# Two transformer blocks on one core: a 512-column moving operand in the MLP's up projections, and steps moved at the first norm, in the mix stage, at the FFN's end and in the last norm

## The chip, the core and the metric

The kernel runs on one core of a Trainium2 chip. Times are device microseconds of an execution of the whole program. The core's engines are TensorE (PE; its weight loads are shown as PEld), VectorE (DVE), ScalarE (ACT), GpSimd (POOL) and SyncE (SP, which here only issues DMAs). Each runs its own instructions in order and waits for the others by semaphores.

## The reference, cut to what matters

```python
def reference(x, ...):                       # x is 1 x 256 x 1024, fp32
    h = rms_norm(x, mix_pre_norm)
    mix = hybrid_token_mixer(h, w_in, ...)   # window attention, block attention, gated delta rule
    x = x + rms_norm(mix, mix_post_norm)
    x = x + rms_norm(conv_glu_ffn(rms_norm(x, ffn_pre_norm), ...), ffn_post_norm)   # width 2816
    h = x
    for l in range(2):
        hn = rmsnorm(h, norm_mix_g[l])
        h = h + (gmlp_mixer(hn, ...) if l == 0 else mla_mixer(hn, kv, ...))
        h = h + sq_relu_mlp(rmsnorm(h, norm_mlp_g[l]), mlp_w1[l], mlp_w2[l])
        if l == 0: kv = shared_latent_kv(h, ...)
    return rmsnorm(h, final_norm_g)

def sq_relu_mlp(hn, w1, w2):                 # w1 1024 x 4096, w2 4096 x 1024
    return jnp.square(jax.nn.relu(hn @ w1)) @ w2
def rms_norm(x, w): return x * lax.rsqrt(jnp.mean(x * x, -1, keepdims=True) + 1e-6) * w
```

## The kernel before, in words

**Products in three parts.** Weights and activations are fp32. Each is split into a high part rounded to fp32r, the operand type that TensorE takes in one pass, and a low part that holds the rest: `w = w_hi + w_lo`, `h = hT_hi + hT_lo`. A product is the sum of hi x hi, lo x hi and hi x lo; `mm3` (L240 to L242) issues these three matmuls into one place of PSUM. Smaller products in the attention parts are plain fp32, which the trace shows as two passes for each matmul.

**Units.** All weights stream from HBM in units of 1 MB (128 x 2048 fp32), in three slots (`raw`) that are refilled in turn. `load` on SyncE waits until a slot's unit has been split, `split_hi` (L204) on ScalarE makes w_hi once the unit has landed and TensorE has used the unit three before, and `split_lo` (L218) on VectorE makes w_lo from it. TensorE waits for `lo_ready`.

**Stages.** They are mix, ffn, gmlp, mlp0, mla and mlp1, in this order. The 256 tokens are two blocks of 128. X (tokens on the partitions) is normalized, turned by TensorE into hT (8 tiles of 128 features x 256 tokens), and multiplied. From the second stage on the scale of a norm is applied to the sums afterwards, and only the first and the last norm scale rows themselves: `norm_act`, `norm_dve`, `norm_pool`. At the start ScalarE squares X in four halves (L358), VectorE adds two sums (L390), GpSimd raises the mean to -1/2 (L420, `n_rstd`), and each engine multiplies half of each block (L362, L403). Then ScalarE and VectorE split unit 0 as a whole, and make hT_hi (L382) and hT_lo (L412) tile by tile. PE runs warming matmuls of the identity (`warm`, L329) in its gaps.

**MLP stages** (`plain_pe`, `plain_act`, `plain_dve`; 544 us on and 814 us on). 16 pairs, each of 2 x 128 hidden features. An up unit (`up`, `features`) forms 2 tiles of 128 features x 256 tokens: for each tile 8 k steps of `mm3` with 256 columns of hT, 48 matmuls, both tiles in the halves of one bank. ScalarE takes the relu (L701), VectorE squares it (L731, act_f), ScalarE rounds act_hi (L706), VectorE makes act_lo (L736). A down unit (`down`) adds the pair's part to four banks (ACC) with 24 matmuls of 512 columns; it is run one pair later, behind the next up unit, for which TensorE waits on `pair_lo`. The splits of two weight units stand between these steps on ScalarE and VectorE. Pairs 2 to 13 run in loops of three pairs.

**Mix stage.** Its units are named by what they project: QB, K0, K1, ZB, KB, VB and so on. SyncE loads QB, K0 and K1 as units 0 to 2; ZB (unit 3) brings 8 more columns, 1,024 pieces of 32 bytes. `first_taps` on ScalarE (it needs `par`, the transposed parameters) and `other_taps` on VectorE (L2221) are the convolution of a key unit, `silu` closes it (L2075), and `rows_out` (L1788) turns the keys back. GpSimd issues the DMAs of masks, small parameters and the alibi table. Later the levels of a triangular inverse run on TensorE (`products`, L1798) among projections and attention groups: `at_scale` multiplies probabilities (ScalarE, L2059), `at_turn` transposes them; `zs` holds the gate z. L1938 sums the squared queries: 8 matmuls of 8 columns.

**Borders.** `ffn_act`'s `ending` is the last pair of the FFN; after it come `post_act` (L509), `post_dve` (L523, L528, L534) and `post_pool` (L516), the norm of the FFN's output. `final_dve` (L930) scales the last rows and `final_sync` writes them.

## Time and profile before

| | us |
|---|---|
| median of 3 runs | 991.94 (989.93 to 992.95) |
| profiled execution | 990.83 |
| its span, first to last instruction | 989.0 |
| TensorE busy in the span | 968.7 |
| VectorE busy | 641.3 |
| ScalarE busy | 500.6 |
| HBM read | 163.26 MB |

The mean granted clock of TensorE is 0.997. Busy is the union of an engine's instructions; a printed duration of a matmul reaches until its end, while the next one starts earlier, so costs are read from start to start. In a row of the timeline, `[0.52 <-ACT union L2171]` is the idle time before it and what ended it; `x4` is a number of merged instructions. 128x256 is partitions x elements per partition.

### The profile page before, as it was taken

The page shows a single profiled execution, that of the slowest core. Times are in us where ns is not written, and L with a number is a line of the kernel's source. Part 1 is how long each engine was busy: PE and PEld are TensorE (multiplying, and loading weights), DVE is VectorE, ACT ScalarE, POOL GpSimd, SP SyncE. Part 2 cuts the span into 40 slices and gives each one's busy share as a digit, 9 for nine tenths or more (in the row PEclk, how much of TensorE's full clock was granted, in tenths as well). Part 3 has the DMA queues.
Part 4 walks back from the last instruction along what each step waited for, and adds up shares of the span by engine and source line. Part 5 has one row for each costly group of instructions (what it writes and reads, how often), then busy time and mean ns, then how long its engine had stood idle before and what let it go on. Part 6 is the DMA issues. An engine that isn't in the chain of part 4 may idle for free.

```text
span 989.0 us, 16482 instructions
## 1 busy us (share of the span) xinstructions
PE 968.7 (98%) x6739; PEld 901.2 (91%) x6739; DVE 641.3 (65%) x803; ACT 500.6 (51%) x666; POOL 35.1 (4%) x46
## 2 busy tenths in 40 slices
PE   7999999999999999999999999999999999999996
PEld 7999998899999998999999999999899899999995
DVE  5666757687777777587668654555767665454553
ACT  5765464565454556444336434434656464434432
POOL 1000001200000000000001000001000000000000
PEclk9999999999999999999999999999999999999998
DMA  9933213466565545555455565655464446565641
GB/s 280 246 114 122 85 44 96 148 226 213 170 205 177 183 158 155 186 170 171 171 170 184 183 200 177 205 170 186 124 159 171 128 145 218 178 203 176 206 129 42
DMA packets 128590, 165.04 MB, mean 167 GB/s; under 512 B 20862, under 2 KB 111419, under 8 KB 128411
## 3 DMA queue, kind: packets, MB, share of 16 engines
q1 hardware_dynamic: 127067, 159.57, 50.1%
q0 software_dynamic: 1312, 4.68, 1.6%
q8 instruction: 37, 0.61, 0.2%
q14 instruction: 14, 0.11, 0.0%
q10 hardware_dynamic: 160, 0.07, 0.0%
HBM read 163.26 MB, written 1.05 MB: 166 GB/s over the span
## 4 chain that ended last, share of the span: by engine, by line
PE 90%; DVE 4%; ACT 2%; DMA 2%; issue 1%; POOL 0%; POOLq 0%; SPq 0%; DVEq 0%; ACTq 0%
PE ps L240 27%; PE ps L241 27%; PE ps L242 27%; PE ps L1798 2%; PE ps L1177 1%; DMA raw<-in_w_in_dram 1%; DVE w_lo L218 1%; PE ps L1198 1%; ACT w_hi L204 1%; PE ps L1064 1%; PE ps L1793 1%; DVE union L2221 1%; PE ps L451 1%; PE ps L1187 0%; DMA X<-in_x_dram 0%
## 5 line engine op out<-in xcount | busy, mean ns | idle before, releaser
L218 DVE TENSOR_TENSOR w_lo<-raw,w_hi 128x2048 fp32r<-128x2048 f32 (+2 forms) x149 | 338.9, 2276 | 164.2 <-ACT w_hi L204 164.2
L204 ACT ACTIVATE w_hi<-raw 128x2048 fp32r<-128x2048 f32 (+2 forms) x149 | 283.3, 1902 | 137.6 <-PE ps L242 130.4
L240 PE MATMUL ps<-hT_hi,w_hi 128*128 128x256 f32 x1192 | 339.7, 285 | 2.0 <-DVE hT_lo L412 1.6
L241 PE MATMUL ps<-hT_hi,w_lo 128*128 128x256 f32 x1192 | 337.2, 283 | 0.0
L242 PE MATMUL ps<-hT_lo,w_hi 128*128 128x256 f32 x1192 | 337.2, 283 | 0.0
L240 PEld LDWEIGHTS ps<-hT_hi,w_hi 128*128 128x128 f32 x1192 | 228.4, 192 | 4.6 <-issue 1.3
L241 PEld LDWEIGHTS ps<-hT_hi,w_lo 128*128 128x128 f32 x1192 | 228.5, 192 | 1.7
L242 PEld LDWEIGHTS ps<-hT_lo,w_hi 128*128 128x128 f32 x1192 | 228.4, 192 | 0.0
L240 PE MATMUL ps<-w_hi,act_hi 128*128 128x512 f32 x416 | 163.3, 392 | 0.0
L241 PE MATMUL ps<-w_hi,act_lo 128*128 128x512 f32 x416 | 162.4, 390 | 0.0
L242 PE MATMUL ps<-w_lo,act_hi 128*128 128x512 f32 x416 | 162.0, 389 | 0.0
L242 PEld LDWEIGHTS ps<-w_lo,act_hi 128*128 128x128 f32 x416 | 78.1, 188 | 16.7
L240 PEld LDWEIGHTS ps<-w_hi,act_hi 128*128 128x128 f32 x416 | 78.3, 188 | 14.9
L241 PEld LDWEIGHTS ps<-w_hi,act_lo 128*128 128x128 f32 x416 | 78.3, 188 | 14.4
L240 PE MATMUL ps<-w_hi,hT_hi 128*128 128x256 f32 (+3 forms) x256 | 81.1, 317 | 2.0 <-DVE hT_lo L412 0.8
L242 PE MATMUL ps<-w_lo,hT_hi 128*128 128x256 f32 (+3 forms) x256 | 79.2, 309 | 0.0
L241 PE MATMUL ps<-w_hi,hT_lo 128*128 128x256 f32 (+3 forms) x256 | 79.1, 309 | 0.0
L701 ACT ACTIVATE act_tmp<-ps 128x512 f32<-128x512 f32 x32 | 19.1, 598 | 108.7 <-PE ps L242 108.7
L731 DVE TENSOR_TENSOR act_f<-act_tmp 128x512 f32<-128x512 f32 x32 | 22.1, 691 | 58.3 <-ACT act_tmp L701 58.3
L240 PEld LDWEIGHTS ps<-w_hi,hT_hi 128*128 128x128 f32 x256 | 48.8, 190 | 5.3 <-issue 2.4
L242 PEld LDWEIGHTS ps<-w_lo,hT_hi 128*128 128x128 f32 x256 | 48.7, 190 | 2.7
L241 PEld LDWEIGHTS ps<-w_hi,hT_lo 128*128 128x128 f32 x256 | 48.8, 191 | 2.2
(298 smaller groups left out, 899.6 us busy)
## 6 DMA issues: line engine op xcount, KB each, us to landing
raw<-in_mlp_w_dram SPq DMA_DIRECT2D x64, 1024.0 KB, 5.3
raw<-in_w_up_dram SPq DMA_DIRECT2D x22, 1024.0 KB, 5.1
raw<-in_a_w_in_dram SPq DMA_DIRECT2D x16, 1024.0 KB, 5.3
raw<-in_w_in_dram SPq DMA_DIRECT2D x12, 1024.0 KB, 6.6
raw<-in_w_down_dram SPq DMA_DIRECT2D x11, 1024.0 KB, 4.9
raw<-in_a_w_out_dram SPq DMA_DIRECT2D x8, 1024.0 KB, 4.8
raw<-in_w_out_dram SPq DMA_DIRECT2D x4, 1024.0 KB, 5.0
raw<-in_b_w_o_dram SPq DMA_DIRECT2D x4, 1024.0 KB, 5.0
```

The source lines that it names most:

```text
L204: nc.scalar.activation(w_hi[:, s, 0:n], raw[:, r, 0:n], ACT.Copy).then_inc(hi_ready, 1)
L218: nc.vector.tensor_tensor(w_lo[:, s, 0:n], raw[:, r, 0:n], w_hi[:, s, 0:n].bitcast(F32), ALU.subtract).then_inc(lo_ready, 1)
L240: nc.tensor.matmul(o, a[0], b[0], start=start, stop=False, skip_group_check=shared)
L241: nc.tensor.matmul(o, a[1], b[0], start=False, stop=False, skip_group_check=shared)
L242: return nc.tensor.matmul(o, a[0], b[1], start=False, stop=stop, skip_group_check=shared)
L451: mm = pe.transpose(turned(n, t)[:, tb * P:(tb + 1) * P], X[:, tb, t * P:(t + 1) * P], ident[:])
L701: nc.scalar.activation(act_tmp[:, m, :], W[m][:], func).then_inc(f.t, 1)
L731: nc.vector.tensor_tensor(act_f[:, m, :], act_tmp[:, m, :], by, ALU.mult).then_inc(f.f, 1)
L1064: mm = nc.tensor.matmul(W[3][:, t * S + tb * P:t * S + (tb + 1) * P], gv[:, tb, c:c + P], wsT[:, p, :], start=True, stop=True)
L1177: mm = nc.tensor.matmul(o, qs[m], ks[m], start=m == 0, stop=m == len(qs) - 1)
L1198: mm = nc.tensor.matmul(o, gr.v(h, kb), PT[:, kb, h, :], start=kb == 0, stop=kb == gr.tb)
L1798: mm = nc.tensor.matmul(bank[:, hs], a[:, g, :], b[:, g, :], start=True, stop=True)
```

## The change

It has six parts.

1. **Up units of the MLP.** hT_hi and hT_lo lie side by side for each tile (`hT[:, k, 0 or 1, :]`), so that both are one moving operand of 512 columns. `up_halves` runs, for each k, w_lo x hT_hi of 256 columns for tile 0 and for tile 1, then w_hi x [hT_hi, hT_lo] of 512 columns for tile 0 and for tile 1. A tile has a bank of its own, and successive matmuls go to the two banks in turn. A bank's left half holds hi x hi, its right half the rest. ScalarE copies the right half, VectorE adds the left one, and one operation takes relu and square. The pairs run in loops of six (SyncE's too). Pair 0 is computed as before.
2. **First norm and unit 0.** ScalarE squares and scales block 0, VectorE block 1, 1024 wide; GpSimd adds epsilon. Unit 0 comes in two DMAs of 4 k tiles and is split by halves, as unit 1 is; units 0 and 1 are multiplied k by k (`up_by_tile`). 8 warming matmuls on zeros stand ahead of the identity's arrival.
3. **Start of the mix stage.** ScalarE loads the silu table by a 1-element activation; the parameter copy and the first taps stand ahead of the splits of ZB and KB; VectorE's taps stand ahead of them too. ZB's narrow DMA is issued ahead of its wide one. GpSimd's DMAs wait for ZB and KB.
4. **Inverse's products.** The 8 sums of squared queries go one by one among the last products, behind waits for the squares and the probabilities' copies; `at_scale` of the last group moves behind the squares and the copy of zs.
5. **FFN's end.** `split_hi(act, u + 4)` stands ahead of the two act_hi copies.
6. **Last norm.** VectorE multiplies halves 0 to 2 by the gains as they close; then the scales are applied by both engines, and four DMAs of half a block write the result, one from ScalarE's queue. The last down unit takes `down_by_block`'s order.

The core of the diff:

```diff
+        def up_halves(b, u):
+            w_h, w_l = weights(u, KT)
+            for k in range(KT):
+                for t in range(PAIR):
+                    nc.tensor.matmul(banks[:, b + t, S:2 * S], w_l[:, k, t * P:(t + 1) * P], hT[:, k, 0, :], start=k == 0, stop=False,
+                                     skip_group_check=True)
+                for t in range(PAIR):
+                    mm = nc.tensor.matmul(banks[:, b + t, :], w_h[:, k, t * P:(t + 1) * P], hT[:, k, :, :].rearrange("p x s -> p (x s)"),
+                                          start=False, stop=k == KT - 1, skip_group_check=True)
+            mm.then_inc(unit_used, 1)
...
+        def mlp_act(act, f, n, extra=None):
...
+                    nc.scalar.copy(tiles2(act_tmp, m % 3), banks[:, b:b + 2, S:2 * S]).then_inc(f.t, 1)
+                if not last:
+                    split_hi(act, u + 3, 2 * i)
...
+        def mlp_dve(dve, f, n, extra=None):
...
+                    nc.vector.tensor_tensor(tiles2(act_tmp, m % 3), banks[:, b:b + 2, 0:S], tiles2(act_tmp, m % 3),
+                                            ALU.add).then_inc(f.z, 1)
...
+                    nc.vector.scalar_tensor_tensor(act_f[:, m % 3, :], z, 0.0, z, ALU.max, ALU.mult).then_inc(f.f, 1)
...
+        def start_norm_dve(dve, gain):
...
+            half_split_lo(dve, 0, 0)
+            dve.wait_ge(g_ok, 1)
+            norm_lo(dve, 0, gain, tiles=range(0, 4))
+            half_split_lo(dve, 0, 1)
+            norm_lo(dve, 0, gain, tiles=range(4, KT))
+            half_split_lo(dve, 1, 0)
+            half_split_lo(dve, 1, 1)
...
+                split_hi(act, u + 4)
                 for t in range(PAIR):
                     c = slice(t * S, (t + 1) * S)
                     act.wait_ge(f.f, j + 1 + t)
                     nc.scalar.copy(act_hi[:, m, c], g[:, c]).then_inc(f.hi, 1)
-                split_hi(act, u + 4)
...
-            pool.wait_ge(landed[1], landed_at[1])
+            pool.wait_ge(landed[ZB % RAW], landed_at[ZB])
...
-            pool.wait_ge(landed[2], landed_at[2])
+            pool.wait_ge(landed[KB % RAW], landed_at[KB])
...
+            def products_and_sums(bank, a, b, tb, done, first):
+                for h, g, hs in heads(tb):
+                    mm = nc.tensor.matmul(bank[:, hs], a[:, g, :], b[:, g, :], start=True, stop=True)
+                    if first == h // 2:
+                        sums = nc.tensor.matmul(ps[6][:, 8 * g:8 * g + 8], sqT[:, h, tb * P:(tb + 1) * P], onec[:], start=True, stop=True)
...
             nc.scalar.copy(qbT, ps[0][:].rearrange("p (t s) -> p t s", t=2)).then_inc(e_p, 1)
+            nc.scalar.activation(stat[:, 15:16], stat[:, 0:1], ACT.Silu)
+            start_act(act)
+            first_taps(0, False)
             split_hi(act, u0 + QB + 3)
-            start_act(act)
-            first_taps(0)
+            split_hi(act, u0 + K0 + 3)
             first_taps(1)
...
-            at_scale(act, gs[3])
             act.wait_ge(d_si, 3)
             nc.scalar.activation(sqT, qT, ACT.Square).then_inc(d_si, 1)
             act.wait_ge(unit_used, u0 + Z1 + 1)
             nc.scalar.copy(zs[:, :, UC:2 * UC], ps[1][:].rearrange("p (b c) -> p b c", b=TB)).then_inc(e_p, 1)
+            at_scale(act, gs[3])
```

On TensorE, at the head of an up unit in a loop of the first MLP, the program had these rows (ps2 is a bank, `pair_t` the relu of the pair before):

```order
L240 MATMUL ps2<-hT_hi,w_hi 128x256 [waits pair_t]
L241 MATMUL ps2<-hT_hi,w_lo 128x256
L242 MATMUL ps2<-hT_lo,w_hi 128x256
L240 MATMUL ps2<-hT_hi,w_hi 128x256
L241 MATMUL ps2<-hT_hi,w_lo 128x256
```

In the changed kernel the same place reads (`ps` is now one tensor of all eight banks):

```order
L863 ISA [waits lo_ready]
L851 MATMUL ps<-hT,w_lo 128x256 [waits pair_f]
L851 MATMUL ps<-hT,w_lo 128x256
L854 MATMUL ps<-hT,w_hi 128x512 x2
L851 MATMUL ps<-hT,w_lo 128x256 x2
L854 MATMUL ps<-hT,w_hi 128x512 x2
```

Three matmuls of 256 columns for a tile and k became one of 256 and one of 512, tile 0 and tile 1 in turn.

On VectorE, at the start of the program, from the first norm to the second unit's low part, before:

```order
L390 SCALAR_TENSOR_TENSOR stat<-stat 128x1 [waits n_sq]
L403 TENSOR_SCALAR XN<-X,stat 128x512 [waits n_rstd]
L390 SCALAR_TENSOR_TENSOR stat<-stat 128x1 [waits n_sq]
L403 TENSOR_SCALAR XN<-X,stat 128x512 [waits n_rstd]
L218 TENSOR_TENSOR w_lo<-raw,w_hi 128x2048 [waits hi_ready]
L412 SCALAR_TENSOR_TENSOR hT_lo<-ps4,par,hT_hi 128x256 [waits n_hi,g_ok]
```

and in the changed kernel:

```order
L401 SCALAR_TENSOR_TENSOR act_tmp,stat<-X 128x1024 [waits x_in1]
L404 TENSOR_SCALAR XN<-X,stat 128x1024 [waits n_rstd]
L248 TENSOR_TENSOR w_lo<-raw,w_hi 128x1024 [waits half_hi]
L491 SCALAR_TENSOR_TENSOR hT<-ps,par,hT 128x256 [waits n_hi,g_ok]
L491 SCALAR_TENSOR_TENSOR hT<-ps,par,hT 128x256 [waits n_hi] x3
L248 TENSOR_TENSOR w_lo<-raw,w_hi 128x1024 [waits hi_ready]
L491 SCALAR_TENSOR_TENSOR hT<-ps,par,hT 128x256 [waits n_hi] x4
```

The first hT_lo tile (L412, now L491) stands behind half of unit 0's low part, the second half between tiles 3 and 4.

On VectorE behind the last matmul, before (ps6 and ps7 are the sums of the second block, L501 closes the residual):

```order
L501 SCALAR_TENSOR_TENSOR X<-ps6,stat,X 128x512 [waits acc_done]
L501 SCALAR_TENSOR_TENSOR X<-ps7,stat,X 128x512 [waits unit_used]
L390 SCALAR_TENSOR_TENSOR stat<-stat 128x1 [waits n_sq]
L930 SCALAR_TENSOR_TENSOR act_tmp<-X,stat,rows 128x1024 [waits n_rstd,rows_in]
L930 SCALAR_TENSOR_TENSOR act_tmp<-X,stat,rows 128x1024 [waits n_rstd]
```

and in the changed kernel (L581 closes the residual):

```order
L581 SCALAR_TENSOR_TENSOR X<-ps,stat,X 128x512 [waits acc_done]
L581 SCALAR_TENSOR_TENSOR X<-ps,stat,X 128x512 [waits unit_used]
L446 TENSOR_TENSOR act_tmp<-X,rows 128x512 [waits x_done]
L450 SCALAR_TENSOR_TENSOR stat<-stat 128x1 [waits n_sq]
L465 TENSOR_SCALAR act_tmp<-act_tmp,stat 128x512 [waits o_z,n_rstd]
L467 SCALAR_TENSOR_TENSOR act_tmp<-X,stat,rows 128x512 [waits n_rstd]
```

One 512-wide operation (L467) stands behind the second power where a 1024-wide one (L930) stood.

## Rows read from the trace of the kernel before

**Rows 1.** The page's part 1 (busy time) and part 4 (chain by engine).

```profile
PE 968.7 (98%) x6739; PEld 901.2 (91%) x6739; DVE 641.3 (65%) x803; ACT 500.6 (51%) x666; POOL 35.1 (4%) x46
...
PE 90%; DVE 4%; ACT 2%; DMA 2%; issue 1%; POOL 0%; POOLq 0%; SPq 0%; DVEq 0%; ACTq 0%
```

**Rows 2.** First MLP: length; busy PE, PEld, DVE, ACT, POOL; PEclk, DMA share, GB/s.

```profile
544.00:689.00 145.00, 145.00 (x934) 132.69 (x933) 79.39 (x63) 62.81 (x52) 0.22 (x1) 1.00 0.58 188
```

**Rows 3.** Timeline of TensorE, first MLP: start us, us, engine, line, operation.

```profile
600.22 0.28 PE L240 MATMUL ps<-hT_hi,w_hi 128*128 128x256 f32 x1
...
605.98 0.40 PE L240 MATMUL ps<-w_hi,act_hi 128*128 128x512 f32 x1
...
611.44 0.28 PE L240 MATMUL ps<-hT_hi,w_hi 128*128 128x256 f32 x1
...
695.74 0.40 PE L240 MATMUL ps<-w_hi,act_hi 128*128 128x512 f32 x1
...
705.29 0.92 PE L451 MATMUL ps<-ident,X 128*128 128x128 f32 x7
```

**Rows 4.** Timeline of ScalarE and VectorE beside that pair.

```profile
606.17 0.60 ACT L701 ACTIVATE act_tmp<-ps 128x512 f32<-128x512 f32 x1 [3.84 <-PE ps L242]
...
606.67 1.91 ACT L204 ACTIVATE w_hi<-raw 128x2048 fp32r<-128x2048 f32 x1
...
606.80 0.69 DVE L731 TENSOR_TENSOR act_f<-act_tmp 128x512 f32<-128x512 f32 x1 [2.14 <-ACT act_tmp L701]
...
608.61 2.29 DVE L218 TENSOR_TENSOR w_lo<-raw,w_hi 128x2048 fp32r<-128x2048 f32 x1 [1.11 <-ACT w_hi L204]
...
610.82 0.68 DVE L736 TENSOR_TENSOR act_lo<-act_f,act_hi 128x512 fp32r<-128x512 f32 x1
```

**Rows 5.** Weight transfers (L187) from 810 to 970 us: issue to landing.

```profile
DMA to landing us min/median/max: 4.8/5.2/7.6
```

**Rows 6.** The chain of waits at the start: start us, us, what.

```profile
0.74 3.90 DMA X<-in_x_dram
...
9.11 0.72 ACT XN L362
...
11.73 2.30 DVE w_lo L218
...
14.49 13.99 DMA raw<-in_w_in_dram
```

**Rows 7.** Timeline of TensorE and GpSimd at the start.

```profile
5.38 2.93 PE L329 MATMUL ps<-ident 128*128 128x128 f32 x12
...
11.47 2.40 PE L329 MATMUL ps<-ident 128*128 128x128 f32 x20
...
14.56 0.36 PE L240 MATMUL ps<-hT_hi,w_hi 128*128 128x256 f32 x1 [0.69 <-DVE hT_lo L412]
...
40.45 1.09 PE L1788 MATMUL ps<-ident,union 128*128 128x128 f32 x8 [1.47 <-ACT union L2075]
...
43.49 0.24 POOL L1757 TENSOR_SCALAR dd<-dd 128x8 f32<-128x8 f32 x1 [27.42 <-DVE dd L2245]
```

**Rows 8.** As rows 2, from 40 to 180 us, the mix stage.

```profile
40.00:180.00 140.00, 138.74 (x1096) 130.95 (x1097) 93.73 (x160) 78.44 (x146) 7.50 (x6) 1.00 0.35 108
```

**Rows 9.** Timeline of TensorE late in the mix stage.

```profile
134.44 0.66 PE L1788 MATMUL ps<-ident,union 128*128 128x128 f32 x4 [0.52 <-ACT union L2171]
...
142.34 1.95 PE L1938 MATMUL ps<-onec,XN 128*128 128x8 f32 x16
```

**Rows 10.** Timeline at the end of the FFN.

```profile
368.93 2.29 DVE L218 TENSOR_TENSOR w_lo<-raw,w_hi 128x2048 fp32r<-128x2048 f32 x1 [1.39 <-ACT w_hi L204]
...
370.15 0.19 ACT L509 ACTIVATION_READ_ACCUMULATOR act_tmp<-ps 128x1 f32 x1
```

**Rows 11.** Timeline behind the last matmul.

```profile
983.13 1.53 POOL L420 TENSOR_TENSOR stat<-stat,mhalf 128x1 f32<-128x1 f32 x1 [2.09 <-DVE stat L390]
...
984.69 1.28 DVE L930 SCALAR_TENSOR_TENSOR act_tmp<-X,stat,rows 128x1024 f32<-128x1024 f32 x1 [0.44 <-POOL stat L420]
```

More of the change, by code:

```diff
@@ L649, in __init__ @@
                     self.r = pair_r if st == "gmlp" else None
+                    self.z = pair_z
+                    self.zbase = sum(f.pairs - 1 for n, f in before.items() if n != "gmlp")
         def each_pair(eng, f, per, step, u_of, ending=None):
             bodies = (f.pairs - 2) // per
-            looped = bodies if bodies > 2 else 0
+            looped = bodies if bodies * per > 6 else 0
             step(1, 1, u_of(1), 0)
@@ L688, in plain_pe @@
             else:
-                down(u, (tiles2(act_hi, m), tiles2(act_lo, m)), last=True)
+                down_by_block(pe, u, (tiles2(act_hi, m), tiles2(act_lo, m)))
         def plain_act(act, f, per, func, n, extra=None):
@@ new lines, in mlp_pe, with step @@
+        def mlp_pe(pe, f, n):
+            def step(j, m, u, i):
+                one = isinstance(j, int) and j == 1
+                pe.wait_ge(lo_ready, u + 1 + 2 * i * PERIOD)
+                if not one:
+                    pe.wait_ge(f.f, f.base + j - 1)
+                up_halves(2 * (m % 2), u)
+                pe.wait_ge(f.lo, f.base + j)
+                pe.wait_ge(lo_ready, u + 2 + 2 * i * PERIOD)
+                down(u + 1, (tiles2(act_hi, (m - 1) % 3), tiles2(act_lo, (m - 1) % 3)), first=one)
+            each_pair(pe, f, 6, step, lambda j: f.u0 + 2 * j - 1)
+            u = f.u0 + 2 * f.pairs - 1
+            acts = (tiles2(act_hi, (f.pairs - 1) % 3), tiles2(act_lo, (f.pairs - 1) % 3))
+            pe.wait_ge(f.lo, f.base + f.pairs)
+            pe.wait_ge(lo_ready, u + 1)
+            if n + 1 in UNSCALED:
+                down_by_half(pe, u, acts, n + 1)
+            else:
+                down_by_block(pe, u, acts)
@@ L2523, in _ @@
                 else:
[L2524 to L2525 removed]
+                    split_lo(dve, SPL - 1)
                 if st == "mix":
```

327 lines of the change are left out of this document (205 added, 122 removed).

## The prediction

> **What bounds the kernel now.** I read the page's first part and its chain first. TensorE is busy 98% of the span and the chain that ended last runs on it for 90% [rows 1]: outside a few borders a change pays only if it takes TensorE's own time, and at a border it pays what it takes from the chain. So I asked three things: what one matmul costs from start to start inside the two MLP stages, whether the other engines have room there, and what stands on the chain at the first norm, in the mix stage, at the end of the FFN and after the last matmul.
>
> The MLP stages have no holes. From 544 to 689 us TensorE is busy 145.00 of 145.00 us at a granted clock of 1.00, its 2.4 GHz level [rows 2]. One pair takes 11.22 us (600.22 to 611.44): an up unit of 48 matmuls of 256 columns in 5.76 us, then a down unit of 24 of 512 columns in 5.46 us [rows 3]. Start to start that is 119.9 ns at 256 columns and 227.6 ns at 512. Twice the columns cost 107.7 ns more, so 256 columns are 107.7 ns and 12.2 ns stand on every matmul whatever its width. The printed durations (0.28 and 0.39 us) hold the part that overlaps the next matmul and are not used.
>
> **The wide operand.** Per tile and k the change runs one matmul of 256 columns and one of 512 in place of three of 256: 32 matmuls in an up unit for 48, over the same 12,288 columns. 16 x 119.9 + 16 x 227.6 ns = 5.56 us for 5.76: 0.20 us less. Pairs 1 to 15 of each stage use it (pair 0 keeps the old form), so 30 x 0.20 = 5.9 us go. That the two widths are mixed, and that every matmul goes to another bank than the one before, no row shows. The nearest rows: in a down unit the bank changes after every third matmul (227.6 ns), in the last unit of a stage after every sixth. The 42 matmuls from 695.74 to 705.29 us take 9.55 us [rows 3]; less 5.46 for the first 24, the 18 others take 227.1 ns each. One changes bank in 1 of 3, the other in 1 of 6, for 0.5 ns: at most 3 ns a change, 960 changes, 2.9 us. On the other side a cost of 12.2 ns that vanished wherever the bank changes would give 960 x 12.2 = 11.7 us more. I take no effect, the value of the rows that lie together, and keep 3.0 and 17.6 us gained as the ends of this term.
>
> The Trainium skill, "TensorE: Matmul & The Clock Gate", section "Wait — 56ns, not 53.3ns?", speaks against this edit: it puts the fixed cost of a warm matmul at about 2.5 ns, by which 480 fewer matmuls would be worth 1.2 us in all. The trace has 12.2 ns, nearly five times that (the section measured bf16 matmuls, these read fp32r), so the measurement decides.
>
> **Who must keep up.** A tile's product now lies in two halves of a bank, so ScalarE copies one half (before: relu of all, 0.60 us) and VectorE adds the other and then squares: one more VectorE operation a pair, 0.69 us by L731 [rows 4]. VectorE needs 2 x 2.29 + 0.69 + 0.68 = 6.0 of 11.2 us a pair and gets 6.7 of 11.0. The added one is hidden: ScalarE's split of the next weights (L204, from 606.67, 1.91 us) runs meanwhile and its act_hi copy stands behind it, so act_lo still ends 5.4 us after the unit (611.5), and TensorE asks for it only at 617.2, behind the next up unit. In the last pair no split stands between: 0.60 + 0.69 + 0.75 + 0.61 + 0.68 = 3.3 us, against a down unit of 5.46. Weights land in 4.8/5.2/7.6 us (least, median, most) [rows 5], two transfers in 11.0 us. Loops of six pairs in place of three: units start 11.22 us apart across the old loop's ends too, so that is worth nothing.
>
> **First norm and unit 0.** X's first block lands at 4.64 us; four squares, two powers, two half-wide multiplications (the last until 9.83), then w_hi and w_lo (2.30) of the whole unit 0 [rows 6], hT_lo tiles only behind them, and the first product at 14.56 [rows 7]. New: ScalarE has block 0. One square of 1024 (about 1.25), an added GpSimd sum (0.24, as L1757 [rows 7]) and a power (0.56): rstd at 6.9; its multiplication of 1024, 0.72 and a little over half again, ends at 8.1. VectorE has block 1, landed near 6.1: 1.28 for the square (1024 wide, as L930 [rows 11]), GpSimd 0.9, multiplication 0.9: 9.2, where the old one ended at 9.83. Half of unit 0 is split by ScalarE from 8.1 to 9.2 and by VectorE from 9.3 to 10.5; the first hT_hi tile ends at 10.8, its hT_lo at 11.2, and tiles follow every 0.4 us while TensorE wants one every 0.72. VectorE's second half stands between tiles 3 and 4 and ends near 13.7; TensorE needs it at 11.3 + 2.9 = 14.2. So the first product moves from 14.56 to about 11.3: 3.3 us. Unit 1 (split by halves, the first until 16.6; unit 0 ends at 17.1) and unit 2 (until 20.1, needed at 22.9) stay in time.
>
> TensorE's clock matters here: the first 12 warming passes take 0.22 us each (half rate, the 1.2 GHz level), the 20 from 11.47 us 0.12 (full) [rows 7]. New warming passes begin near 1 us, so I take the full level from about 8; if it comes at 11, the turns end 1.4 us later and the term is 2.0.
>
> Behind it TensorE waits 1.47 us at 40.45 for the silu of the keys [rows 7]. Its cause is the DMA: unit 3 takes 13.99 us to land [rows 6], since GpSimd's table and alibi transfers run beside its 1,024 pieces of 32 bytes, and ScalarE waits for it until 28.48 with the parameter copy and the first taps queued behind. Now those stand ahead of the split, VectorE's taps ahead of its own, the silu table is loaded early, and GpSimd's transfers wait until units 3 and 4 have landed. I put unit 3 near 22 us against a need at 24.5. Unit 2 is multiplied by 28.9, ZB's w_lo ends at 29.2 and its products at 35.6, the keys' silu at 33: the 1.47 goes. 3.3 + 1.5 = 4.8; I take 4.6, for a chain this long seldom loses nothing. Ends: 1.5 (a late clock and a late unit 3) and 5.5.
>
> **Mix.** ScalarE's scaling of the last probabilities now stands behind the square of the queries and the copy of zs, for which TensorE waits 0.52 us at 134.44 [rows 9]. The copy comes 1.7 us earlier and the scaling, done near 134.1, is just in time for the turn: 0.5. The 16 passes of query sums (1.88 us from 142.34, 117 ns each for 8 columns, so bound by their weight loads) go between the products. The loads stay one to a pass, so I take 0; ends: 1.0 slower (ScalarE's copies of the products start later) and 1.0 faster.
>
> **FFN's end.** VectorE's w_lo, from 368.93 until 371.2, keeps L523 from its first product, whose square was there at 370.34 [rows 10]. The split now goes into ScalarE's idle time from 364.2, so w_lo ends near 369.8, L523 starts 0.8 us earlier, and the two means and closings behind it, for which TensorE waits, 0.5. It delays the first act_hi copy by 0.8, to 366.5; act_lo, at 367.0, is still there before TensorE ends the unit ahead. Ends 0 and 0.8.
>
> **Last norm.** The last data is ready at 984.69 + 1.28 = 985.97 [rows 11]. Now the gains are multiplied in early, and behind the second power stand one 512-wide VectorE operation (0.7) and one on ScalarE. The last closing moves to 982.5 (0.4 later, three operations ahead of it), the last square ends at 983.3, the power at 984.1 to 984.5 (it took 1.53 us beside L930), the last half at 985.1: 0.9, and a transfer is half as large: 1.0. Ends 0.2 and 1.6.
>
> **Sum.** 5.9 + 4.6 + 0.5 + 0.5 + 1.0 = 12.5 us. The profiled execution took 990.83 us (span 989.0 and 1.8 around it), which gives 978.3; the median of the runs shown, 991.94, is 1.1 above it: 979.4.
>
> **Rivals.** A: the start's gain is given back before the FFN, the mix being a weave of TensorE, VectorE and ScalarE steps whose units load only when their slots are split. Against: from 40 to 180 us TensorE is busy 138.74 of 140 us [rows 8], so little else leads. If half or all of it goes: 981.7 to 984. B: a wide matmul costs two narrow ones when mixed with them, 239.8 ns, and the edit brings nothing: 979.4 + 5.9 = 985.3. Against: 24 in a row take 227.6 each. The skill's 2.5 ns, named above, would end nearly there, at 984.1. C: alternating banks removes the fixed cost: 979.4 - 11.7 = 967.7; the 3 ns point the other way. D, slower: a matmul into another bank than its predecessor's waits for it. Place: the 960 of the wide units. It takes 13 ns a change to undo the whole gain and 16 to be seen as slower; at 20 ns the time is 979.4 + 19.2 = 998.6. For it is only that no row has a change at every matmul; against it, 3 ns a change. E: the second half of unit 0 or unit 3 comes late and the wide units bring nothing either: 990.
>
> **Chances.** Forecast 0.63, A 0.17, B 0.06, C 0.07, D 0.03, E 0.04. About 0.3%, 3 us, can be told from no change here. Faster by more: 0.63 + 0.17 + 0.06 + 0.07 = 0.93; same 0.04; slower 0.03. The range holds the forecast's own (976 to 982.5), A's and nearly B's: 975 to 985.
>
> **What would show it.** Right: pairs of 11.02 us in both MLP stages with TensorE busy throughout, starts 120 and 228 ns apart; the first product near 11.3 us and no wait ahead of the keys' turns, none for zs; the FFN's L523 no longer behind w_lo; the last output operation 0.9 us nearer to the last matmul. Wrong: a pair above 11.15 or below 10.9, TensorE waiting for pair_lo or for weights inside an MLP stage, a first product after 12.5 us, or a mix stage that is longer than before from the keys' turns to its last unit.

## The result, and the profile after

The changed kernel takes 978.19 us (median, 978.03 to 978.42) against 991.89 us (989.93 to 992.95) for the kernel before, timed beside it: a ratio of 0.987 (95% interval 0.986 to 0.988). Forecast were 979.4 us and 975 to 985. The profiled execution took 978.03 us, its span is 976.0: 13.0 us shorter.

Page of the changed kernel, parts 1 and 4, to be laid beside [rows 1]:

```profile
PE 961.9 (99%) x6269; PEld 874.1 (90%) x6269; DVE 663.4 (68%) x838; ACT 500.4 (51%) x664; POOL 34.8 (4%) x48
...
PE 95%; DVE 2%; ACT 1%; issue 1%; DMA 0%; POOL 0%; POOLq 0%; DVEq 0%; ACTq 0%
```

TensorE lost 470 matmul records and 6.8 us of busy time, VectorE gained 22 us (mostly the added operation, 30 x 0.69), and the chain now runs on TensorE for 95% in place of 90%. Where the 13.0 us went I read by laying the same operation of both timelines side by side: the distance of each pair, and by how much it grew.

| place | before | after | apart | gained there |
|---|---|---|---|---|
| first product | 14.56 | 11.95 | 2.61 | 2.6 |
| keys' turns | 40.45 | 35.95 | 4.50 | 1.9 |
| mix, a `products` of the inverse | 119.63 | 115.07 | 4.56 | 0.1 |
| mix, the turn that waited for zs | 134.44 | 129.21 | 5.23 | 0.7 |
| mix, first `state_out` | 144.22 | 138.58 | 5.64 | 0.4 |
| FFN, last down unit | 361.95 | 356.27 | 5.68 | 0.0 |
| FFN's end, second turn | 376.72 | 370.37 | 6.35 | 0.7 |
| first MLP, its turns | 526.20 | 519.87 | 6.33 | 0.0 |
| its end, the next turns | 705.29 | 695.90 | 9.39 | 3.1 |
| second MLP, last down unit but one | 970.24 | 957.86 | 12.38 | 3.0 |
| end of the span | 989.0 | 976.0 | 13.0 | 0.6 |

**Inside the MLP.** The stretch of [rows 2] in the changed kernel (length; busy PE, PEld, DVE, ACT, POOL; PEclk, DMA share, GB/s), and the heads of two up and two down units, to be laid beside [rows 3]:

```profile
544.00:689.00 145.00, 145.00 (x738) 123.31 (x737) 92.14 (x74) 65.26 (x57) 3.69 (x1) 1.00 0.58 190
```

```profile
603.71 0.40 PE L851 MATMUL ps<-hT,w_lo 128*128 128x256 f32 x2
...
609.28 0.39 PE L270 MATMUL ps<-w_hi,act_hi 128*128 128x512 f32 x1
...
614.72 0.40 PE L851 MATMUL ps<-hT,w_lo 128*128 128x256 f32 x2
...
620.30 0.39 PE L270 MATMUL ps<-w_hi,act_hi 128*128 128x512 f32 x1
```

An up unit takes 5.57 to 5.58 us for 5.76, a down unit 5.44 for 5.46, a pair 11.01 for 11.22, without a hole. Beside them ScalarE's copy, VectorE's addition and square, and the split, in the place of [rows 4]:

```profile
598.47 0.59 ACT L888 COPY act_tmp<-ps 128x512 f32<-128x512 f32 x1 [3.66 <-PE ps L854]
598.95 1.92 ACT L219 ACTIVATE w_hi<-raw 128x2048 fp32r<-128x2048 f32 x1
599.09 0.69 DVE L912 TENSOR_TENSOR act_tmp<-ps,act_tmp 128x512 f32<-128x512 f32 x1 [1.95 <-ACT act_tmp L888]
599.82 0.69 DVE L916 SCALAR_TENSOR_TENSOR act_f<-act_tmp 128x512 f32<-128x512 f32 x1
...
603.11 0.69 DVE L920 TENSOR_TENSOR act_lo<-act_f,act_hi 128x512 fp32r<-128x512 f32 x1
```

act_lo is there at 603.8 us, TensorE asks for it at 609.28: the added operation is hidden with 5.5 us to spare.

**The start.** Timeline of ScalarE, VectorE, GpSimd and TensorE, for [rows 6, 7]:

```profile
5.35 2.27 PE L361 MATMUL ps<-ident 128*128 128x128 f32 x18
...
6.10 1.23 DVE L401 SCALAR_TENSOR_TENSOR act_tmp<-X 128x1024 f32<-128x1024 f32 x1 [5.06 <-DMA X<-in_x_dram]
6.38 1.38 POOL L420 TENSOR_TENSOR stat<-stat,mhalf 128x1 f32<-128x1 f32 x1
...
7.79 1.15 ACT L391 ACTIVATE XN<-X,stat 128x1024 f32<-128x1024 f32 x1 [1.84 <-POOL stat L420]
...
8.15 0.57 POOL L420 TENSOR_TENSOR stat<-stat,mhalf 128x1 f32<-128x1 f32 x1
...
9.08 1.94 PE L546 MATMUL ps<-ident,XN 128*128 128x128 f32 x16 [1.46 <-ACT XN L391]
...
11.95 0.35 PE L270 MATMUL ps<-hT,w_hi 128*128 128x256 f32 x1
```

The first of two equal powers takes 1.38 us, the second 0.57. The granted clock is at its full level, 2.4 GHz, from 4.44 us (a pass behind it takes 0.126 us); in the kernel before it was there from 11.27.

**The tail.** Timeline behind the last matmul, for [rows 11]:

```profile
970.94 0.49 DVE L465 TENSOR_SCALAR act_tmp<-act_tmp,stat 128x512 f32<-128x512 f32 x1
971.09 0.73 POOL L497 TENSOR_TENSOR stat<-stat,mhalf 128x1 f32<-128x1 f32 x1 [1.70 <-DVE stat L450]
...
971.86 0.75 DVE L467 SCALAR_TENSOR_TENSOR act_tmp<-X,stat,rows 128x512 f32<-128x512 f32 x1 [0.44 <-POOL stat L497]
972.61 0.39 ACTq L440 DMA_DIRECT2D out_dram<-act_tmp  x1
972.64 0.33 SPq L1110 DMA_DIRECT2D out_dram<-act_tmp  x1
```

The last data is ready at 972.61, 13.36 us earlier than at 985.97, but the span ends 3.39 us behind it where it ended 3.03 behind. The trace has the landing of the last transfer 2.92 us after its issue (972.64 to 975.56, 256 KB, with those issued at 971.85 and 972.61 still under way); before, it was 2.64 (986.01 to 988.64, 512 KB, alone).

### The profile page after: what moved, and what is told of

The parts are those of the page before. It is cut to its first block, busy times and chain, and to the rows that moved or that the text cites. A ratio compares the mean times of both kernels' runs of the same rounds, so it can differ in the third digit from the quotient of the medians.

```text
span 976.0 us, 15567 instructions
## 1 busy us (share of the span) xinstructions
PE 961.9 (99%) x6269; PEld 874.1 (90%) x6269; DVE 663.4 (68%) x838; ACT 500.4 (51%) x664; POOL 34.8 (4%) x48
## 3 DMA queue, kind: packets, MB, share of 16 engines
HBM read 163.26 MB, written 1.05 MB: 168 GB/s over the span
## 4 chain that ended last, share of the span: by engine, by line
PE 95%; DVE 2%; ACT 1%; issue 1%; DMA 0%; POOL 0%; POOLq 0%; DVEq 0%; ACTq 0%
PE ps L270 23%; PE ps L272 22%; PE ps L271 22%; PE ps L854 11%; PE ps L851 6%; PE ps L1972 2%; PE ps L1351 2%; PE ps L1372 1%; PE ps L1967 1%; PE ps L1238 1%; PE ps L532 1%; PE ps L1361 0%; PE ps L2101 0%; DMA X<-in_x_dram 0%; PE ps L2121 0%
## 5 line engine op out<-in xcount | busy, mean ns | idle before, releaser
L233 DVE TENSOR_TENSOR w_lo<-raw,w_hi 128x2048 fp32r<-128x2048 f32 x147 | 334.3, 2276 | 133.7 <-ACT w_hi L219 133.7
L219 ACT ACTIVATE w_hi<-raw 128x2048 fp32r<-128x2048 f32 x147 | 279.9, 1904 | 129.7 <-PE ps L272 128.4
L270 PE MATMUL ps<-hT,w_hi 128*128 128x256 f32 x712 | 203.7, 286 | 1.4 <-DVE hT L491 0.9
L271 PE MATMUL ps<-hT,w_lo 128*128 128x256 f32 x712 | 201.4, 283 | 0.0
L272 PE MATMUL ps<-hT,w_hi 128*128 128x256 f32 x712 | 201.4, 283 | 0.0
L854 PE MATMUL ps<-hT,w_hi 128*128 128x512 f32 x480 | 150.8, 395 | 0.0
L270 PEld LDWEIGHTS ps<-hT,w_hi 128*128 128x128 f32 x712 | 136.4, 192 | 2.8 <-issue 1.5
L271 PEld LDWEIGHTS ps<-hT,w_lo 128*128 128x128 f32 x712 | 136.5, 192 | 0.6
L272 PEld LDWEIGHTS ps<-hT,w_hi 128*128 128x128 f32 x712 | 136.4, 192 | 0.0
L851 PEld LDWEIGHTS ps<-hT,w_lo 128*128 128x128 f32 x480 | 90.0, 188 | 20.9
L851 PE MATMUL ps<-hT,w_lo 128*128 128x256 f32 x480 | 94.5, 278 | 0.0
L270 PE MATMUL ps<-w_hi,hT 128*128 128x256 f32 (+3 forms) x256 | 81.1, 317 | 1.9 <-DVE hT L491 0.8
L272 PE MATMUL ps<-w_lo,hT 128*128 128x256 f32 (+3 forms) x256 | 79.2, 309 | 0.0
L271 PE MATMUL ps<-w_hi,hT 128*128 128x256 f32 (+3 forms) x256 | 79.1, 309 | 0.0
L854 PEld LDWEIGHTS ps<-hT,w_hi 128*128 128x128 f32 x480 | 73.1, 189 | 0.0
L888 ACT COPY act_tmp<-ps 128x512 f32<-128x512 f32 x30 | 17.7, 589 | 100.4 <-PE ps L854 100.4
```

Source lines behind the costliest of these rows:

```text
L219: nc.scalar.activation(w_hi[:, s, 0:n], raw[:, r, 0:n], ACT.Copy).then_inc(hi_ready, 1)
L233: nc.vector.tensor_tensor(w_lo[:, s, 0:n], raw[:, r, 0:n], w_hi[:, s, 0:n].bitcast(F32), ALU.subtract).then_inc(lo_ready, 1)
L270: nc.tensor.matmul(o, a[0], b[0], start=start, stop=False, skip_group_check=shared)
L271: nc.tensor.matmul(o, a[1], b[0], start=False, stop=False, skip_group_check=shared)
L272: return nc.tensor.matmul(o, a[0], b[1], start=False, stop=stop, skip_group_check=shared)
L851: nc.tensor.matmul(banks[:, b + t, S:2 * S], w_l[:, k, t * P:(t + 1) * P], hT[:, k, 0, :], start=k == 0, stop=False, skip_group_check=True)
```

## The experiments

All are edits of the changed kernel and compute the same output. Times are medians; runs 5 to 8 have one execution each. The changed kernel was timed in the first set only. The kernel before was timed beside every set, and its median lay between 990.30 and 991.89 us, so differences below about 1 us are read from the traces and not from the times.

**1. Narrow matmuls again, all else kept (`e1_narrow`).**

```diff
-                    mm = nc.tensor.matmul(banks[:, b + t, :], w_h[...], hT[:, k, :, :]...)
+                for x in range(2):
+                    for t in range(PAIR):
+                        mm = nc.tensor.matmul(banks[:, b + t, x * S:(x + 1) * S], w_h[...], hT[:, k, x, :], ...)
```

> The changed kernel, but in the MLP's wide up units the one matmul of 512 columns (w_hi x [hT_hi, hT_lo]) is two of 256, into the left and the right half of the same bank; tiles, banks, copies, additions, splits and order stay: 48 matmuls a unit for 32, the same 12,288 columns, and nearly every matmul still goes to another bank than the one before. Theory F (a fixed cost of about 12.2 ns on each matmul): a pair takes 11.22 us again for 11.02, 30 pairs, +5.9 us: 978.2 + 5.9 = 984.1, TensorE without holes. Rival B' (the 5.9 us came from another part of the change, for instance from the loops of six pairs or from the two banks): pair stays 11.02 us, 978.2. Rival D' (changing the bank at each matmul costs time that the wide form hid): pair above 11.3 us, over 986.5.

984.24 us (983.92 to 984.37). Heads of two up units and the down unit between them:

```profile
605.05 0.40 PE L851 MATMUL ps<-hT,w_lo 128*128 128x256 f32 x2
...
610.80 0.40 PE L270 MATMUL ps<-w_hi,act_hi 128*128 128x512 f32 x1
...
616.27 0.40 PE L851 MATMUL ps<-hT,w_lo 128*128 128x256 f32 x2
```

A pair is 11.22 us again (up 5.75, down 5.47), so the step of the width alone is worth 6.1 us. The loops of six, the two banks and the other form of relu and square together are worth nothing. B' and D' are out.

**2. One bank after the other (`e2_one_bank`).**

```diff
-            for k in range(KT):
-                for t in range(PAIR): (w_lo, 256 columns)
-                for t in range(PAIR): (w_hi, 512 columns)
+            for t in range(PAIR):
+                for k in range(KT): (w_lo, 256 columns), (w_hi, 512 columns)
```

> The changed kernel, but the MLP's wide up units run tile 0 over all eight k (256 and 512 columns in turn, all into one bank) and then tile 1 into the other bank: one change of bank in 32 matmuls in place of one at nearly every matmul; same matmuls, same number. Theory F (bank does not matter, the cost is per matmul and per column): pair 11.02 us, 978.2 within 0.6. Rival C' (alternating banks saves a part of the gain): pair longer, by up to 0.20 us, up to 984. Rival D' (alternating banks costs): pair shorter, by up to 3 ns x 32 = 0.10 us, down to 975.3.

980.95 us (980.68 to 981.18): +2.8. Heads of two units, TensorE's timeline:

```profile
604.93 0.28 PE L851 MATMUL ps<-hT,w_lo 128*128 128x256 f32 x1
...
610.57 0.40 PE L270 MATMUL ps<-w_hi,act_hi 128*128 128x512 f32 x1
...
616.03 0.28 PE L851 MATMUL ps<-hT,w_lo 128*128 128x256 f32 x1
```

The up unit takes 5.64 us, the pair 11.11: nearly half of the gain is lost to an order of the same 32 matmuls. Theory F (only number and columns count) falls. It looked like C', but two things had changed together: the bank, and that 256 and 512 columns now alternate at every matmul (in the changed kernel they come two and two). Runs 9 to 11 part them.

**3. 384 and 128 columns for 512 (`e3_uneven`).**

```diff
-                    mm = nc.tensor.matmul(banks[:, b + t, :], w_h[...], hT[:, k, :, :]...)
+                for c in (slice(0, 384), slice(384, 512)):
+                    for t in range(PAIR):
+                        mm = nc.tensor.matmul(banks[:, b + t, c], w_h[...], hh[:, c], ...)
```

> The changed kernel, but the wide matmul of 512 columns is one of 384 and one of 128 (a up unit has then 16 matmuls of 256, 16 of 384 and 16 of 128 columns: 48, and 12,288 columns). From 119.9 ns at 256 and 227.6 ns at 512 columns two readings are possible. Theory F (12.2 ns on each matmul + 0.421 ns a column): 119.9 + 173.8 + 66.1 = 359.7 ns a tile and k, the same as three of 256: pair 11.22 us, time 984.1. Rival L (a matmul takes at least as long as its weight load, near 117 ns by the query sums, and 256 columns happen to lie near that floor): 119.9 + 173.8 + 117 = 410.7 ns, unit 6.57 us, pair 12.03, +30 us: about 1008.5. Between the two, a smaller floor: the pair's length gives the price of 128 columns.

1006.15 us (1006.04 to 1006.74): 28.0 us more than the changed kernel, and 21.9 more than run 1, which has as many matmuls and columns. Head of an up unit and of the next down unit:

```profile
610.24 0.40 PE L851 MATMUL ps<-hT,w_lo 128*128 128x256 f32 x2
...
616.65 0.45 PE L270 MATMUL ps<-w_hi,act_hi 128*128 128x512 f32 x1
```

6.41 us for 16 groups of 256, 384 and 128 columns: 400.6 ns each. Less 119.9 and 173.8 (interpolated) that leaves 106.9 ns for 128 columns, where the line through 256 and 512 gives 66. So rival L holds in kind, and the trace shows where: from 560 to 680 us no two weight loads of TensorE (its rows PEld) start less than 107 ns apart, close to the 117 ns a pass of the query sums [rows 9]. It is a floor of the loads, not of each matmul. Start to start the first of two matmuls of 128 columns takes 60 ns and the second 111, and the first of 256 columns behind them 164 for 119.9: short matmuls leave the next loads uncovered. At 256 columns the floor lies just below. The line 12.2 ns + 0.421 ns a column is good from 256 to 512 columns (384 take 174.6 here, 173.8 by the line), and not below. The down units of this run are also 0.1 us longer (5.54); why, no run tells.

**4. Another division of the first norm (`e4_swap`).**

```diff
-            act.wait_ge(n_rstd, 1)
-            nc.scalar.mul(XN[:, 0, :], X[:, 0, :], stat[:, 6:7]).then_inc(n_xa, 1)
+            act.wait_ge(x_in[1], 16)
+            nc.scalar.activation(act_tmp[:, 2:4, :]..., X[:, 1, :], ACT.Square, ..., accum_out=stat[:, 2:3]).then_inc(n_sv, 1)
...
-            nc.vector.scalar_tensor_tensor(act_tmp[...], X[:, 1, :], 1.0 / D, X[:, 1, :], ...)
+            dve.wait_ge(n_rstd, 1)
+            nc.vector.tensor_scalar(XN[:, 0, :], X[:, 0, :], stat[:, 6:7], None, ALU.mult).then_inc(n_xa, 1)
```

> The changed kernel with another division of the first norm: ScalarE squares both blocks (block 1 where it multiplied block 0), VectorE squares none and multiplies both blocks by their scales (tensor_scalar, 0.75 us each for ScalarE's 1.15). Theory P (GpSimd's power took 1.38 us for 0.57 because it stood blocked until VectorE's square of block 1, an operation with two SBUF inputs, ended at 7.34): the first power takes about 0.57 us again and ends at 6.95, XN of block 0 is there at 7.7 (8.94 before), block 1's at 9.0 (9.5), w_hi of unit 0 starts at 7.4 (8.85), the first product comes near 10.9 us for 11.95, and about 1.0 us of it reaches the end: 977.2 (976.8 to 977.9). Rival Q (the first power is slow by itself, as the first of its kind or through what GpSimd loads): it stays at 1.38 us, XN of block 0 at 8.5, first product 11.5, 977.8. Rival R (the time ahead of ZB is set by DMA landings, so nothing of it lasts): first product earlier, the keys' turns still at 35.95, 978.2.

978.00 us (977.33 to 978.25): nothing that can be told from 978.19. Its timeline shows why:

```profile
5.35 4.21 PE L361 MATMUL ps<-ident 128*128 128x128 f32 x18
...
6.39 0.57 POOL L420 TENSOR_TENSOR stat<-stat,mhalf 128x1 f32<-128x1 f32 x1
6.99 0.75 DVE L402 TENSOR_SCALAR XN<-X,stat 128x1024 f32<-128x1024 f32 x1 [5.94 <-POOL stat L420]
...
9.08 1.06 ACT L242 ACTIVATE w_hi<-raw 128x1024 fp32r<-128x1024 f32 x1 [0.45 <-DMA raw<-in_w_in_dram]
...
9.35 2.07 PE L546 MATMUL ps<-ident,XN 128*128 128x128 f32 x16
```

P is right on the power (0.57 us) and Q is out: XN of block 0 is ready at 7.74. But two waits took its place. In this execution the granted clock came to 2.4 GHz only at 9.66 us, so the 18 warming passes took 4.21 us, and the turns stood behind them; and unit 0's second half lands at 9.08, with hT_hi queued behind its w_hi on ScalarE. The first product came at 12.07.

**5 and 6. The power alone; unit 0's low part in one piece (`e5_lone_power`, `e6_whole_unit0`).**

```diff
+            dve.wait_ge(n_rstd, 1)                  # 5: ahead of VectorE's square
```
```diff
             half_split_lo(dve, 0, 0)
+            half_split_lo(dve, 0, 1)                # 6: both halves ahead of the tiles
...
-            half_split_lo(dve, 0, 1)                # (it stood between tiles 3 and 4)
```

> The changed kernel with one wait more: VectorE's square of block 1 waits until GpSimd's first power is done. Read at that place only. Theory P (the power is blocked by VectorE's two-input operation): the power takes about 0.57 us for 1.38, rstd of block 0 is there at 6.95 for 7.76; VectorE's square runs 7.0 to 8.2, the second sum and power follow to 9.1, XN of block 1 ends at 9.9 (9.5 in the changed kernel), XN of block 0 at 8.1 (8.94). The first product near 11.5 to 12. Rival Q (slow by itself): the power keeps its 1.38 us and all stands 1.2 us later.

> The changed kernel, but VectorE makes both halves of unit 0's low part ahead of the first hT_lo tile (before: the second half between tiles 3 and 4). Theory: the tiles start one half-split (1.21 us) later, the first product at 13.1 to 13.2 us for 11.95, and from there all is 1.2 us later until the keys' turns (37.1 for 35.95): about 979.4 in this one look. Rival (VectorE is not what the first product waits for): 11.95 stays.

Run 5: 977.99 us. With one wait more the power takes 0.57 us:

```profile
6.43 0.57 POOL L421 TENSOR_TENSOR stat<-stat,mhalf 128x1 f32<-128x1 f32 x1
7.03 1.15 ACT L391 ACTIVATE XN<-X,stat 128x1024 f32<-128x1024 f32 x1 [1.03 <-POOL stat L421]
7.11 1.23 DVE L402 SCALAR_TENSOR_TENSOR act_tmp<-X 128x1024 f32<-128x1024 f32 x1 [6.07 <-POOL stat L421]
```

The square only moves behind it, block 1 comes later, and the first product stays (11.93).

Runs whose start is not edited show the same blocking in a second form. In the changed kernel the addition ahead of the power starts at 6.07 us and VectorE's square at 6.10: the addition takes 0.22 us, the power 1.38. In runs 3, 8, 10 and 11 the square starts first, by 0.01 to 0.03 us, and the addition takes 1.27 to 1.30 us and the power 0.57. The scale of block 0 is then there at 7.81 to 8.30 us for 7.76, and the first product comes at 12.01 to 12.49. So a start can differ by some tenths of a us between executions for this reason alone.

Run 6: 978.96 us. TensorE waits for hT_lo:

```profile
12.94 0.36 PE L270 MATMUL ps<-hT,w_hi 128*128 128x256 f32 x1 [0.90 <-DVE hT L491]
```

The first product comes 0.99 us later and the keys' turns, at 36.93, 0.98. Of this 0.11 was there with the first power (7.87 for 7.76), so splitting by halves is worth 0.9 us, and it lasts to the keys' turns.

**7. GpSimd's transfers early again (`e7_gpsimd_dmas_early`).**

```diff
-            pool.wait_ge(landed[ZB % RAW], landed_at[ZB])
+            pool.wait_ge(landed[1], landed_at[1])
-            pool.wait_ge(landed[KB % RAW], landed_at[KB])
+            pool.wait_ge(landed[2], landed_at[2])
```

> The changed kernel, but GpSimd's transfers wait for units 1 and 2 as in the kernel before, and no longer for ZB and KB (units 3 and 4). Theory T (they slowed unit 3's 1,024 pieces of 32 bytes, 13.99 us to land): unit 3 lands at 24 to 28 us for 20.95, ScalarE's w_hi of ZB starts then and not at 25.14, ZB's first product moves from 30.04 to up to 33, and about 1 to 3 us are lost. Rival U (the new order of the splits alone took the wait for the silu away, and the table and alibi transfers were harmless): unit 3 lands by 25.1, ZB's first product stays at 30.04, the time too.

981.45 us, +3.3. What was waited for from 12 to 40 us (in total, times, longest), two rows of its waits:

```profile
ACT w_hi L219 <- DMA raw<-in_w_in_dram: 3.3, 2, 2.3
...
PE ps L270 <- DVE w_lo L233: 2.3, 1, 2.3
```

In the changed kernel these are 1.3 and 0.3. ZB's w_hi starts at 27.55 us for 25.14, its first product at 31.96 for 30.04, the keys' turns at 39.40 for 35.95. T is right and U is out, but only 1.92 of the 3.45 us are the landing. Behind the wait of 2.3 us the granted clock fell to 0.50, the 1.2 GHz level, from 33.49 to 36.90 us, and ZB's matmuls started 0.22 us apart for 0.12:

```profile
34.17 0.42 PE L270 MATMUL ps<-w_hi,hT 128*128 128x264 f32 x1
34.39 0.42 PE L271 MATMUL ps<-w_hi,hT 128*128 128x264 f32 x1
```

That is the other 1.53 us; the changed kernel's clock stays up there. From the first product to the keys' turns it is 25.89 us before, 24.00 in the changed kernel, and 27.47 here, or 25.94 without the fallen clock. So by this reckoning the new order of the splits alone would have gained nothing, and the 1.9 us behind the first product hang on these two waits of GpSimd.

**8. Three steps put back (`e8_moves_back`).** at_scale ahead of zs's copy; the sums behind the products; in the FFN:

```diff
-                split_hi(act, u + 4)
                 for t in range(PAIR): (the act_hi copies)
+                split_hi(act, u + 4)
```

> The changed kernel with three steps put back, far enough apart to be read each in its own stretch: the query sums behind all products, the last at_scale ahead of the squares and of the copy of zs, and in the FFN split_hi of the next unit behind the act_hi copies. Expected by my terms: 0.5 us lost at the second turn of the mix stage near 129 us, 0 at the query sums by the prediction, 0.3 to 0.4 by what the changed kernel's trace shows between 132.3 and 138.6 us; 0.7 us lost at the FFN's end between 356 and 372 us; in all 1.5 us, 979.7. Rival: the FFN's 0.7 came from the wide banks' turns and not from the split, then nothing is lost there.

980.23 us. The start was 0.36 us late here, so each step is read in its own stretch. TensorE, first this kernel, then the changed one:

```profile
130.24 0.66 PE L1962 MATMUL ps<-ident,union 128*128 128x128 f32 x4 [0.52 <-ACT union L2354]
133.40 3.74 PE L1972 MATMUL ps<-union 128*128 128x128 f32 x32
138.14 1.95 PE L2118 MATMUL ps<-onec,XN 128*128 128x8 f32 x16
140.02 1.09 PE L2124 MATMUL ps<-union 128*64 128x128 f32 x8
```

```profile
129.21 0.60 PE L1962 MATMUL ps<-ident,union 128*128 128x128 f32 x4
132.30 0.39 PE L2101 MATMUL ps<-union 128*128 128x128 f32 x2
132.53 0.29 PE L2103 MATMUL ps<-onec,XN 128*128 128x8 f32 x2
...
138.58 1.04 PE L2121 MATMUL ps<-union 128*64 128x128 f32 x8
```

The wait for zs is back at 0.52 us (0.7 with what follows it). From the products to `state_out` it is 6.62 us for 6.28: weaving the sums in is worth 0.34. At the FFN's end the wait for X grows from 0.29 to 0.97, 0.68 us. Together 1.7 of the 13.0, where 1.5 was expected.

**9 to 11. Which order of the 32 matmuls (`e9_pairs_by_tile`, `e10_grouped_one_bank`, `e11_narrow_first`).** N is a matmul of 256 columns, W of 512, the digit the tile and its bank:

```
changed     N0 N1 W0 W1  per k
one bank    N0 W0        per k, then N1 W1 per k
9           N0 W0 N1 W1  per k
10          8 x N0, 8 x W0, 8 x N1, 8 x W1
11          8 x (N0 N1), 8 x (W0 W1)
```

> Why 32 matmuls of a wide unit take 5.64 us when each tile stays in one bank (one-bank kernel, pair 11.11 us), and 5.57 us in the changed kernel (11.02). Here, for each k: tile 0's 256 columns, tile 0's 512, tile 1's 256, tile 1's 512. So the width changes at every matmul, as in the one-bank kernel (in the changed one at every second), and the bank at every second (one-bank: once in 32; changed: at nearly each). Theory W (a change of width costs, near 5 ns each): pair 11.11 us, time 980.9. Theory K (a matmul into its predecessor's bank costs): half of the matmuls pay, pair 11.06, 979.5.

> Tile 0: its eight matmuls of 256 columns, then its eight of 512, all into one bank; then tile 1. No bank change within a tile, and the width changes 3 times in 32 matmuls. Theory W (the change of width costs): pair 11.00 to 11.02 us or a little less, time 977.5 to 978.2. Theory K (the predecessor's bank costs): pair 11.11 us, 980.9 as the one-bank kernel.

> The sixteen matmuls of 256 columns for both tiles first, tiles (and banks) in turn, then the sixteen of 512, in turn: one change of width a unit, a bank change at every matmul. Theory W: the best order, pair at most 11.00 us, time 977.4 to 978.2. Theory K: as the changed kernel, pair 11.02, 978.2.

| | us | pair | up unit | bank changes, width changes a unit |
|---|---|---|---|---|
| changed | 978.19 | 11.013 | 5.573 | 31, 15 |
| one bank (2) | 980.95 | 11.107 | 5.645 | 1, 31 |
| 9 | 980.91 | 11.107 | 5.645 | 15, 31 |
| 10 | 978.58 | 11.026 | 5.587 | 1, 3 |
| 11 | 978.00 | 11.007 | 5.567 | 31, 1 |

(Pairs as means over 9 to 11 pairs of each trace.) One change of bank or fifteen make no difference in the alternating order, and grouped in one bank nearly all of the 0.09 us is back. So it is the alternation of widths that costs, and the bank next to nothing: 0.02 us a unit between 10 and 11, 0.6 ns a matmul. But W in its simple form (5 ns for each change) fails too: 15 changes cost 0.006 us a unit, 31 cost 0.078. What is dear is one by one: a matmul of 256 and one of 512 columns take 352.9 ns together where single ones alternate (runs 2 and 9), 348.3 in the changed kernel, 349.2 in run 10 and 347.9 in run 11. Which of the two takes the 5 ns no run tells: start to start it is 116.7 and 236.1 ns in runs 2 and 9, 115.2 and 233.1 in the changed kernel. That w_lo and w_hi alternate with the widths is not enough by itself: they change in the kernel before too, at 119.9 ns for 256 columns. What happens stays open.

**12. The version the runs point to (`e12_combined`).** Order 11, the division of run 4, and

```diff
-                    warm(pe, 9)
+                    warm(pe, 5)
             half_split_hi(act, 0, 0)
-            half_split_hi(act, 0, 1)
-            norm_hi(act, 0, gain)
+            norm_hi(act, 0, gain, range(0, 4))
+            half_split_hi(act, 0, 1)
+            norm_hi(act, 0, gain, range(4, KT))
```

> The version that the runs point to: the changed kernel with the MLP's sixteen 256-column matmuls of a unit ahead of its sixteen 512-column ones (pair 11.007 us for 11.013), and at the start: ScalarE squares both blocks, VectorE scales both (the powers take 0.57 us each), 5 warming matmuls of the identity for 9 (10 passes for 18, so that they end by 7.7 us even at half rate), and ScalarE makes w_hi's second half of unit 0 behind the first four hT_hi tiles, since that half's data lands only at 9.08 us. If what held the start back in the swapped version was the late clock behind 18 passes and the landing ahead of hT_hi, the first product comes at 10.9 to 11.1 us for 11.95, the keys' turns at 34.9 to 35.2 for 35.95, and the time is 978.2 - 1.0 - 0.2 = 977.0 (976.7 to 977.4). If the clock falls back for want of warming, turns and first products take 0.23 us and more each, and it is 978 or above. If the landing of VB (ScalarE waits for it until 31.90) or of ZB binds, the turns stay near 35.5: 977.6.

977.37 us (977.10 to 977.99, ratio to before 0.986, 0.985 to 0.988): every execution lies below every one of the changed kernel, but they were timed in another set, and the intervals of the ratios overlap. The first product comes at 11.34 us (0.6 earlier), the keys' turns at 35.70 (0.25 earlier):

```profile
PEld ps L1964 <- ACT union L2255: 0.2, 1, 0.2
```

ScalarE waits 2.5 us for weights ahead of the silu in place of 1.3, and the turns wait for the silu. X's first block landed 0.19 us later in this execution (4.92 for 4.73), and the granted clock rose at 9.47. The third of the expected outcomes is the one that came, at nearly its price: the start is now bound by the landing of VB, for which ScalarE's split waits until 32.69 us (31.90 in the changed kernel).

## Why the prediction was right

979.4 against 978.2 us, and each term has the sign that was forecast. That the sum is so near is in part luck: the terms gave 13.0 us for 12.5, with errors of +0.2, -0.1, +0.6, +0.2 and -0.4 that mostly cancel. The base was worse than the sum. The forecast carried 1.1 us from the profiled execution to the median over from the kernel before, and in the changed kernel the two lie 0.2 apart (978.03 and 978.19). That is most of the 1.2 us by which the forecast was too high. Point by point:

- **Wide operand, 5.9:** 6.1 in the trace, 6.1 by taking it back (run 1). The 12.2 ns from two widths held for the third unit form, 5.57 for 5.56 us. That it held owed something to the order: "I take no effect" was right of the banks (runs 2, 9, 10), but of the alternation of widths, which costs up to 2.8 us, only rival B took account. I had ends of 3.0 and 17.6 for the wrong reason.
- **First norm and start, 4.6:** 4.5. The first product missed: 11.95 for 11.3. The failed step is "GpSimd sum (0.24) and a power (0.56): rstd at 6.9"; the power took 1.38 us, since VectorE's square of block 1 ran beside it, and rstd came at 7.8. Taking that away alone brought nothing back (runs 4 and 5, 12.07 and 11.93): the landing of unit 0's second half and block 1 stand right behind it, and only run 12, which moves these too, has 11.34. The row that warned of it was the 1.53 us in [rows 11], used in the tail but not here. On the other side the part behind it, forecast as 1.5, gave 1.9; that it is GpSimd's transfers is shown (run 7). So 4.5 for 4.6 is two misses that cancel. The clock, feared late, was at its level from 4.44 us, and in run 4 from 9.66.
- **Mix, 0.5:** 1.1. The zs wait went, 0.7 with what follows; the sums, taken at 0, gave 0.34. The failed step is "The loads stay one to a pass, so I take 0". They do, but between products of 128 columns a sum's pass costs less than the 117 ns that it takes among its like: 16 passes in 1.88 us before, about 1.54 woven in, 96 ns each.
- **FFN's end, 0.5:** 0.7 (run 8 gives 0.68).
- **Last norm, 1.0:** 0.6. The last data came 1.0 us nearer, as worked out (0.9). "A transfer is half as large" failed: the last two halves become ready at 972.58 and 972.61 and leave together, 512 KB as before; the last took 2.92 us to land for 2.64, and the span's end stands 0.36 us further behind its data, for 0.1 nearer.
- **VectorE's room, the landings, the loops of six:** as said, no wait inside an MLP stage, pairs 11.22 us in run 1 with loops of six.

The rivals: A (the start's gain given back) did not come, 4.50 at the keys' turns are 4.56 at 115 us. B and D are refuted by the 11.01 us pair, C by the same. B is right in kind, though, for an order that the change doesn't have: where single widths alternate (runs 2 and 9), 2.8 of the 6.1 us go. The trace went against the 2.5 ns of the Trainium skill, "TensorE: Matmul & The Clock Gate", section "Wait — 56ns, not 53.3ns?": taking 480 matmuls away was worth 6.1 us, 12.7 ns each.

## What to carry to other kernels

On fp32r operands count matmuls as well as columns: from 256 to 512 columns each costs 12 ns on top, and one of 128 columns still costs about 107 ns (a pass of 8 columns 117 among its like); put narrow ones side by side and not one by one between wide ones. A small GpSimd operation on the path may last until the wide VectorE operation beside it has ended: look at what VectorE started just before. A wait of TensorE can cost more than itself: the 2.3 us of run 7 were followed by 1.5 us lost to a fallen clock. A step that frees the start is worth what the next landing leaves of it, so look at that first.
